# Attention of a two-layer diffusion step: exponents turned by VectorE blocks and a DMA exchange in place of TensorE transposes

## The reference

```
for each block of 128 queries, each of 4 heads:
    s = (q . k) * scale                  # 128 queries x keys
    p = softmax(s)                       # over the keys
    o = p @ v                            # sum over the keys
```

## Time and profile before

| What | Value |
|---|---|
| Median of 3 runs | 2510.32 us (2508.66 to 2511.09) |
| Span of the profiled execution | 2507.0 us |
| TensorE matmul, busy | 2404.6 us, 96% |
| VectorE busy | 769.9 us, 31% |
| ScalarE busy | 511.8 us, 20% |
| GpSimd (POOL) busy | 276.9 us, 11% |
| DMA, mean of the span | 155 GB/s |
| TensorE's share of the chain that ended last | 92% |

### The profile page before, as it was taken

How to read it: one execution, slowest core, us unless ns; L and a number is a source line. 1 busy time by engine, 2 the same in 40 slices (tenths; PEclk the granted TensorE clock), 3 DMA queues, 4 the chain that set the end, 5 groups by cost and what they waited for, 6 DMA issues and landing times.

```text
span 2507.0 us, 31553 instructions
## 1 busy us (share of the span) xinstructions
PE 2404.6 (96%) x13056; PEld 1591.4 (63%) x13056; DVE 769.9 (31%) x1547; ACT 511.8 (20%) x1048; POOL 276.9 (11%) x434
## 2 busy tenths in 40 slices
PE   6999999999998999999999999999999959999996
PEld 4545556666444878878855455566654447888785
DVE  2401334455237211111142022455533461111113
ACT  3310122222234201101042102222223331011003
POOL 2000011201000111121110000120000002111111
PEclk8999999999999999999999999999999979999998
DMA  9100224301426788888950002310022258888888
GB/s 327 34 14 8 84 74 131 87 13 51 176 101 223 256 276 275 272 279 279 336 187 17 21 0 84 110 43 11 9 74 101 84 202 269 278 272 272 276 282 301
DMA packets 165692, 388.06 MB, mean 155 GB/s; under 512 B 14528, under 2 KB 24952, under 8 KB 165600
## 3 DMA queue, kind: packets, MB, share of 16 engines
q1 hardware_dynamic: 142832, 332.47, 38.6%
q0 software_dynamic: 22768, 54.29, 9.2%
HBM read 339.08 MB, written 47.65 MB: 154 GB/s over the span
## 4 chain that ended last, share of the span: by engine, by line
PE 92%; DVE 3%; SPq 2%; DMA 2%; ACT 1%; issue 1%; DVEq 0%; POOLq 0%; ACTq 0%
PE PS L1380 11%; PE PS L1387 11%; PE PS L1226 11%; PE PS L1412 9%; PE PS L979 8%; PE PS L1072 7%; PE PS L1137 7%; PE PS L933 5%; PE PS L920 4%; PE PS L1119 4%; PE PS L1084 4%; PE PS L1406 2%; PE PS L1033 1%; PE PS L1365 1%; PE PS L1097 1%; PE PS L1018 1%
## 5 line engine op out<-in xcount | busy, mean ns | idle before, releaser
L1380 PEld LDWEIGHTS PS<-r,ring 128*128 128x128 f32 x2048 | 281.5, 190 | 15.2 <-issue 15.2
L1226 PE MATMUL PS<-ring,mix 128*128 128x512 f32 x640 | 288.4, 598 | 1.2 <-DVE mix L1960 1.2
L1380 PE MATMUL PS<-r,ring 128*128 128x160 f32 x2048 | 283.6, 299 | 0.3 <-ACT r L1683 0.2
L1387 PE MATMUL PS<-r,ring 128*128 128x160 f32 x2048 | 283.4, 299 | 0.0
L1387 PEld LDWEIGHTS PS<-r,ring 128*128 128x128 f32 x2048 | 279.9, 190 | 0.0
L1412 PE MATMUL PS<-ring,r 128*128 128x512 f32 x496 | 221.2, 599 | 0.0
L979 PE MATMUL PS<-r,ring 128*128 128x512 f32 (+1 forms) x576 | 208.4, 522 | 1.6 <-ACT r L1504 1.6
L1072 PE MATMUL PS<-lat,r 128*128 128x512 f32 (+1 forms) x416 | 203.6, 587 | 4.8 <-ACT r L1547 2.7
L1226 PEld LDWEIGHTS PS<-ring,mix 128*128 128x128 f32 x640 | 116.6, 190 | 129.6 <-issue 129.5
L1914 DVE COPY r<-PS 128x512 f32<-128x512 f32 x200 | 138.3, 691 | 187.5 <-PE PS L1119 187.4
L1137 PE MATMUL PS<-r 128*128 128x256 f32 x768 | 188.3, 381 | 0.0
(11 more groups left out here) (305 smaller groups left out, 2183.7 us busy)
## 6 DMA issues: line engine op xcount, KB each, us to landing
ring<-in_w_gate_dram SPq DMA_DIRECT2D x32, 2048.0 KB, 10.1
ring<-in_w_up_dram SPq DMA_DIRECT2D x32, 2048.0 KB, 10.7
ring<-in_w_down_dram SPq DMA_DIRECT2D x31, 2048.0 KB, 9.8
ring<-in_w_ada_dram SPq DMA_DIRECT2D x15, 2048.0 KB, 9.8
x_dram<-r SPq DMA_DIRECT2D x20, 512.0 KB, 2.9
r<-x_dram SPq DMA_DIRECT2D x20, 512.0 KB, 4.3
mix<-in_w_ada_dram SPq DMA_DIRECT2D x4, 2048.0 KB, 15.0
r<-in_x_sample_dram SPq DMA_DIRECT2D x16, 512.0 KB, 4.4
```

Of the source, the lines that this page charges most:

```text
L1226: ins = pe.matmul(psum(2 * (s % 2) + n, 512), mix[:, k, tile * P:(tile + 1) * P], W_OUT[n][:, k, :], start=(k == 0), stop=(k == KD - 1))
L1380: ins = pe.matmul(PS[:, b // 2, (b % 2) * 256:(b % 2) * 256 + SLOTS], W_G[:, k, b * P:(b + 1) * P], XST[par][:, k, :], start=(k == 0), sto ...
L1387: ins = pe.matmul(PS[:, 2 + b // 2, (b % 2) * 256:(b % 2) * 256 + SLOTS], W_U[:, k, b * P:(b + 1) * P], XST[par][:, k, :], start=(k == 0), ...
```

## The change

The exponents are no longer turned by TensorE. VectorE turns each slot's exponents in 32x32 blocks, SBUF to SBUF, into PB, one buffer for both slots in ring slot 1. A turned 32x32 block still lies in the partitions of its queries' group, so SP then exchanges the blocks between the four groups of 32 partitions: for each pair (a, b) of groups one DMA from the 32 partitions of group b in PB to the 32 of group a in PTr, 32 rows x 2 slots x 1536 bytes in a full item, 16 DMAs an item. In the moving operand of the product, the 128 queries of a key chunk then lie as four runs of 32. PTr is doubled (pt_landed, one semaphore for each buffer), PB is not: turn_blocks(n, .) waits until the exchange of item n - 1 has landed.

```
-                def turn(n, slot, r):            # TensorE, 4 transposes a round
...
-                def copy_turned(n, slot, r):     # VectorE, PSUM to PTr
...
+                def turn_blocks(n, slot):
+                    x = key_chunks(n) * 32
+                    dve.wait_ge(exp_done, at(l, 2 * NI, 2 * n + slot + 1))
+                    if n:
+                        dve.wait_ge(pt_landed[(n - 1) % 2], at(l, 256 * NI // 2, 256 * ((n - 1) // 2 + 1)))
+                    dve.transpose(PB[slot][:, 0:4 * x].rearrange("p (i c b) -> p c i b", i=4, b=32),
+                                  Pr[slot][:, 0:4 * x].rearrange("p (c i a) -> p c i a", i=4, a=32)).then_inc(p_turned, 1)
...
+                def exchange(n):
+                    x = key_chunks(n) * 32
+                    sp.wait_ge(p_turned, at(l, 2 * NI, 2 * n + 2))
+                    if n >= 2:
+                        sp.wait_ge(o_summed, at(l, NI, n - 1))
+                    for a in range(4):
+                        for b in range(4):
+                            dst = PTr[n % 2][32 * a:32 * a + 32, 0:8 * x].rearrange("p (s i x) -> p s i x", s=2, i=4)
+                            src = ring[32 * b:32 * b + 32, 1, 0:3072].rearrange("p (s x) -> p s x", s=2)
+                            sp.dma_start(dst[:, :, b, :], src[:, :, x * a:x * (a + 1)]).then_inc(pt_landed[n % 2], 16)
+
+                for n in range(NI):
+                    if n < len(ADA_ITEMS[l]):
+                        load_ada(n)
+                    if n == len(ADA_ITEMS[l]):
+                        sp.wait_ge(ada_summed, 1 + ADA_AT[l] + len(ADA_ITEMS[l]) - 1)
+                        unit(2, (W_OUT[0], w_out_src[l, 0]))
+                    if n == len(ADA_ITEMS[l]) + 1:
+                        sp.wait_ge(ada_summed, 1 + ADA_AT[l] + len(ADA_ITEMS[l]))
+                        unit(0, (W_OUT[1], w_out_src[l, 1]))
+                    exchange(n)
```

load_ada(n) holds the five loads of a modulation block, as before. The product takes its exponents from the exchanged buffer, and all of an item's product now runs in iteration n + 2:

```
+                def times_values(n, chunks):
...
+                    if chunks[0] == 0:
+                        pe.wait_ge(pt_landed[n % 2], at(l, 256 * NI // 2, 256 * (n // 2 + 1)))
+                        if n:
+                            pe.wait_ge(o_copied, at(l, NI - 1, n))
...
+                        moving = rows[:, :, :, 32 * c:32 * c + 32]
...
                 for n in range(NI):
                     if n:
                         pe.wait_ge(exp_done, at(l, 2 * NI, 2 * n - 1))
+                    for c in range(3):
+                        scores(n, 0, c)
                     modulation(n - 2)
+                    times_values(n - 2, first_half)
                     if n:
                         pe.wait_ge(exp_done, at(l, 2 * NI, 2 * n))
                     for c in range(3):
                         rotary_scores(n, c)
+                    for c in range(3):
+                        scores(n, 1, c)
+                    turn_modulation(n - 2)
+                    times_values(n - 2, second_half)
```

Behind the loop TensorE does value heads 0 to 2, the product of item 16, heads 3 to 7, the inverses' matmul, heads 8 and 9, the product of item 17, heads 10 and 11. On VectorE an iteration is now:

```
                 for n in range(NI):
                     bias_modulation(n - 2)
+                    divide_out(n - 3)
+                    row_max(n, 0)
+                    row_max(n, 1)
                     copy_modulation(n - 2)
+                    turn_blocks(n, 0)
+                    turn_blocks(n, 1)
+                    if n < NI - 1:
+                        invert_sums(n)
```

More of the change, by code:

```diff
@@ L55, in parts_of, with key_chunks @@
     return 2 if ITEMS[n][1] is PROMPT_TILES else 3
[L58 to L66, removed]
+def key_chunks(n):
+    return 4 if ITEMS[n][1] is PROMPT_TILES else 12
 UV_CHUNKS = [(1, 0), (1, 1), (0, 0), (0, 1), (2, 0), (2, 1), (0, 2), (0, 3), (1, 2), (1, 3), (2, 2), (2, 3)]
 NU = len(UV_CHUNKS)
-def turned(n, slot, r):
-    return ROUND_AT[n] + slot * rounds_of(n) + r + 1
 OUT_ORDER = list(range(PT, NT)) + list(range(PT))
@@ L257, in backbone @@
         Pr = [r2[:, 1536 * i:1536 * (i + 1)] for i in range(2)]
-        PTr = r2[:, 3072:6144].rearrange("p (s k q) -> p s k q", s=2, k=12)
+        PB = [ring[:, 1, 1536 * i:1536 * (i + 1)] for i in range(2)]
+        PTr = [r2[:, 3072 * (i + 1):3072 * (i + 2)] for i in range(2)]
         SHUF = r2[:, 6144:7168]
-        DIAG = r2[:, 6144:6400].rearrange("p (s q) -> p s q", s=2)
-        INV = [r2[:, 7168 + 512 * i:7680 + 512 * i] for i in range(2)]
+        INV = [lat[:, 512 * i:512 * (i + 1)] for i in range(2)]
+        DIAG = lat[:, 1024:1280].rearrange("p (s q) -> p s q", s=2)
         W_A = r2[:, 8192:9216].rearrange("p (h k c) -> p h k c", h=HEADS, k=2)
@@ L365, in backbone @@
         p_turned = sem("p_turned")
-        pt_ready = sem("pt_ready")
+        pt_landed = [sem(f"pt_landed{i}") for i in range(2)]
         o_summed = sem("o_summed")
@@ L519, in _, with load_ada @@
                 sp.wait_ge(ada_zeroed, l + 2)
-                for i, (la, n) in enumerate(ADA_ITEMS[l]):
+                def load_ada(i):
+                    la, n = ADA_ITEMS[l][i]
                     if i >= 2:
@@ L1106, in turn_modulation @@
                     pe.transpose(PS[:, 6, 0:P], ada_s[i % 2], ident[:, :]).then_inc(ada_turned, 1)
-                def turn(n, slot, r):
[L1110 to L1121, removed]
@@ L1123, in times_values @@
-                def times_values(n, r, blocks=range(4)):
-                    if n < 0 or r >= rounds_of(n):
+                def times_values(n, chunks):
+                    if n < 0:
                         return
                     p, t = ITEMS[n]
[L1128 to L1132, removed]
+                    if chunks[0] == 0:
+                        pe.wait_ge(pt_landed[n % 2], at(l, 256 * NI // 2, 256 * (n // 2 + 1)))
+                        if n:
+                            pe.wait_ge(o_copied, at(l, NI - 1, n))
+                    rows = PTr[n % 2][:, 0:256 * key_chunks(n)].rearrange("p (s i x) -> p s i x", s=2, i=4)
+                    for c in chunks:
+                        if c >= key_chunks(n):
+                            continue
+                        moving = rows[:, :, :, 32 * c:32 * c + 32]
@@ L1142, in value_heads @@
+                        if c == key_chunks(n) - 1:
+                            ins.then_inc(o_summed, 1)
                 def value_heads(m):
@@ L1154, in _ @@
                 pe.wait_ge(cond_ready, l + 2)
+                first_half, second_half = range(0, 6), range(6, 12)
                 for n in range(NI):
@@ L1212, in _ @@
                 value_heads(9)
+                times_values(n, range(12))
                 pe.wait_ge(o_divided, at(l, NI, NI))
```

109 lines of the change are left out of this document (26 added, 83 removed).

## The result

| | Before | After |
|---|---|---|
| Median on the same chip | 2509.5 us | 2586.4 us (2583.0 to 2590.4) |
| Ratio, 95% interval | | 1.0305 [1.0291, 1.032] |
| Span of the profiled execution | 2507.0 us | 2584.6 us |

The change makes the kernel 3.05% slower, 77 us. The forecast was 2493 us, 93 us too low, and the time lies outside its range of 2430 to 2565.

What follows compares the result with a forecast made beforehand. TensorE bound the kernel before; afterwards a ring of turns, hand-offs, issues and landing would: 3.8 + 0.1 + 9.6 + 2.0 = 15.5 us a full item. Gains of 13.3 and 4.1 us by layer: 2510.3 - 17.4 = 2493 us, range 2430 to 2565.

Steps and rivals of the forecast that it cites:

- The ring: In attention, block turns, hand-offs, 16 issues and last landing must finish before the next item's turns: 15.5 us a full item.
- Turns, 3.8 us forecast: VectorE's two block turns of 128x1536 in a full item, 1.9 us each, 3.8 us together.
- Issues, 15 x 0.64 = 9.6 us: SP's sixteen exchange issues, 0.64 us apart like the rotary tables: 9.6 us to the start of the last.
- Landing of the last DMA, 2.0 us: An exchange's last 96 KB lands 2.0 us after issue, nearer to a store, with 1.5 and 4.1 as ends.
- POOL's round trip ... stays hidden: POOL's store and load of the inverses take 13.4 us, under the ring's 15.5, so they stay hidden.
- The tail: Layer 0's attention from item 17's rotary to the first output projection: 35.8 us instead of 30.5, a loss of 5.3.
- TensorE's own period, 12.7 us: TensorE's full item without its 24 turns, at most 3.4 us less: 12.7 us, or 15.0 with modulation.
- the -2 us a layer: TensorE, idle some 5 us ahead of landing 17, may run a few matmuls at 1.2 GHz: 2 us lost.
- The landing is dear: Rival, chance 0.33: the exchange's last DMA lands like a load, 4.1 us; ring 17.6 us, time 2569 us.
- POOL's inverses bind: Rival, chance 0.03: POOL's 13.4 us trip grows to 16 and more beside the exchange's packets; about 2510 us.
- Issues are quick: Rival, chance 0.2: SP issues of 0.373 us, ring 11.5 us, TensorE binds at 2405 us; together 2405 to 2450.
- The port rule: 32 partitions reach 8 of 16 ports: 8.3 us an exchange; with short issues a 14.2 us ring, 2446 us.

Runs made afterwards that it cites:

- e1: The changed kernel without POOL's store and broadcast load of the inverses, so it divides by stale numbers; 2509.5 us.
- e7: The changed kernel with full items' inverses spread by a TensorE matmul and copied by ScalarE; only prompt items keep POOL's trips; 2523.7 us.
- e9: e7 with POOL's gate loads held back until the layer's last exchange has landed; 2510.2 us.
- e10: The changed kernel without the broadcast load of the inverses (stale numbers), POOL's store writing contiguous rows instead of single 4-byte elements; 2511.3 us.
- e8: e9 with the exchange's DMAs issued on two queues, SP's and ScalarE's, as in e6; 2441.0 us.
- e13: e12 with the exchange on two queues as in e6 and the gate loads held back as in e9; 2433.8 us.
- e12: The changed kernel with e10's store by rows, the broadcast load kept, and the division reading the inverses with a stride; 2531.5 us.
- e6: The changed kernel with 8 of an exchange's 16 DMAs issued on ScalarE's queue, POOL's trips kept; 2490.3 us.

## Why the prediction was wrong

**The mechanism was right, a size was not.** The ring of block turns, issues and last landing binds, and its length sets the period.
- *Turns, 3.8 us forecast:* 3.44 for two, 1.72 each. That is near the lower end, but the 1.7 that was called the copy's rate does not follow from the row named: three copies of 0.691 us are 2.07. A nearer row stood beside it, the row maximum over the same 128x1536 numbers in 1.753 us.
- *Issues, 15 x 0.64 = 9.6 us:* 9.6, exactly. The rows of the rotary tables, back to back, were the right ones; the single load's 0.373 us would have been wrong, and with it the rival of quick issues.
- *Landing of the last DMA, 2.0 us:* the failed term. 17.9 - 3.44 - 9.6 - 0.1 leaves 4.8 us, 2.8 more than forecast in each of 36 rings; the shorter turns give 0.36 back. As the price of such a DMA by itself 2.0 was right (2.2 in e1, e7, e9 and e10).
- *"POOL's round trip ... stays hidden":* the failed step behind it. Only its length was compared with the ring's (13.4 < 15.5). The length did stay hidden (VectorE's waits ahead of its turns ended on the exchange), but the trip's transfers run beside the exchange's, and I priced them at nothing. e1 measures them: 2586.4 - 2509.5 = 77 us. By what way they hold the exchange up (at a DMA engine, at a port or elsewhere) no run shows.
- *The tail:* forecast -5.3 us a layer from the landings 16 and 17. The gate loads, which I did not list, collide with exchange 16. Once the trips are gone that costs 13.5 us in two layers (e7 against e9). In the changed kernel POOL reaches them later and they cost less there (20.2 and 18.7 us between the last turns, 23.6 and 22.5 in e1), so the trips by themselves cost more than 77; only the sum of the two is measured.
- *TensorE's own period, 12.7 us:* 13.3 (e8, e13). The 0.141 us a turn was named as the most that it could cost and then taken whole; (16.14 - 13.3) / 24 = 0.118 us is what it was worth. This does not touch the forecast, in which the ring binds.

Trips and gate loads account for the miss: 77 + 13.5 = 90.5 of 93 us, and e1 without its gate collision, 2509.5 - 13.5 = 2496 us, is 3 us from the forecast. That it comes so near is partly luck, since smaller errors cancel: 36 x 0.36 = 13 us too much for the turns, against 36 x 0.2 = 7 us too little for the landing and 12 x 0.7 = 8 us for modulated items (costed at nothing with the 2 MB load, with 1 to 2 us as the bound).

**The clock.** TensorE does fall to the lower level behind its waits, more often than the -2 us a layer had it (0.92 in the stretch): half a value product took 4.4 to 4.9 us instead of 2.86 after waits of 6.5, 5.0, 2.3 and 1.9 us, and 2.86 after one of 2.89. It lies beside the ring: the turns of the next item started on their landing (561.27) while this slow product was still under way (561.22 to 566.1).

**The rivals.** "The landing is dear" named 2569 us, and its arithmetic nearly fits; its reason did not hold. An exchange DMA does not land like a DRAM load (4.1 us), but in 2.2 us without POOL's trips. "POOL's inverses bind" was looking at the right neighbour for the wrong effect. "Issues are quick" showed what there was to gain: e13 reaches 2434 us by making the issue term short in another way, on two queues. With TensorE's 13.3 us its 2405 would have been 2510.3 - 32 x 2.8 = 2421 us. The port rule that stood beside it (the Trainium skill, SBUF — State Buffer, Door 1: The DMA port swizzle) was to matter only with short issues. The runs neither show nor refute it. On one queue 96 KB every 0.64 us are 154 GB/s, below the 189 that the rule starts from, so landings of 2.2 us say nothing against it. On two queues an exchange of e8 is issued from 517.9 to 523.1 us, and its last DMA lands 3.1 us later: 1.57 MB in some 8.3 us, as much as the prediction worked out from the rule. Issues and a landing of 2.2 us would be 7.4; whether ports make the rest isn't shown. The ring of 14.2 us counted a landing of 2.0 us on top of the 8.3, and did not come: the plain period of e13 is 13.3 us, and TensorE fills it.

**The signs that were named.** SP's spacing and the nearly equal periods of both kinds of item (17.9 us plain; modulated, the turns of 344.70 to 454.38 us are 109.7 / 6 = 18.3 us apart) came out as listed. TensorE's idle time in front of the value product is released by a DMA, as listed, but is longer, as the ring is: six waits in 330 to 460 us (modulated) make 12.5 us, six in 500 to 620 us (plain) 22.7 us, where near nothing and 2.5 us each were named. The sign about the landing, "about 2 us after the last issue", did not, and on it the sum hung: 1 us a ring is 36 us.

## What to carry to other kernels

When a DMA is put on the path that sets the period, every transfer that runs beside it has to be priced for what it does to that DMA's landing, not only for whether its own result is in time. Tiny DMAs with 4-byte pieces come first: here a store of 1 KB cost 27 to 55 us in 34 executions, and writing the same numbers in the order in which they lie in each partition took that cost away (the broadcast load behind it still cost 20 us in e12). Then spread the issues over two queues, and hold loads that are not urgent until the last critical landing.

## What the runs showed of the hardware

- Sixteen DMAs of 96 KB from SBUF to SBUF, back to back, are issued by SP every 0.64 us; they land 2.2 us after their issue (the median in e1, e7, e9 and e10), and up to 7.2 us after it beside a 1 KB store in 4-byte pieces and a 128 KB broadcast load of POOL's queue.
- That store in 8-byte pieces, with as many packets, lets the exchange land in 2.2 us again (e10), and lands itself in 3.8 us instead of 7.5. Why 4-byte pieces are so much worse isn't settled.
- Eight of the sixteen on ScalarE's queue took 96 us off the time although the landings stayed at 4.6 to 4.8 us (e6).
- VectorE turns 128x1536 float32 numbers in 32x32 blocks in 1.72 us (3.44 us for two), as long as its row maximum over them (1.753 us).
- A 128x128 float32 transpose on TensorE, four in a round between other matmuls, was worth 0.118 us of its time.
